# Dropping four unused columns from the output projection on, and cutting the last three token tiles from the other end

## The chip, the cores and the metric

The kernel runs on one core of a Trainium2 chip, which is trn2. The metric is the device time of one execution in microseconds; the median of three runs is used. The engines are TensorE (PE in the profile, its weight loads PEld), VectorE (DVE), ScalarE (ACT), GpSimd (POOL) and SyncE (SP), which here issues loads and stores.

## What is computed

One inference step of a one-layer encoder, for 1024 prompt tokens and 64 sample tokens that use the same weights. Cut to what matters here:

```
u = RMSNorm(x);  proj = u @ w_in
A = (RG-LRU branch with a width-4 causal conv) @ w_branch_a
B = (mLSTM branch with a width-4 causal conv) @ w_branch_b
x = x + (sigmoid(ga) * A + sigmoid(gb) * B) @ w_out
h = relu(RMSNorm(x) @ w_mlp_up)          # 1024 -> 4096
x = x + (h * h) @ w_mlp_down             # 4096 -> 1024
y = RMSNorm(x)
```

All values are fp32. The causal convolutions look three tokens back, and the sample's convolution starts from a given state.

## The kernel before

Activations lie transposed in SBUF: 128 rows of a feature block on the partitions, tokens as columns. There are KB = 8 feature blocks and COLS = 1092 columns: 1024 prompt tokens, a gap of GAP = 4 that the convolutions need for the sample's state, and 64 sample tokens from column SAMPLE0 = 1028 on. Up to the merge of the two branches every operation works on all 1092 columns, as three thirds of TW = 364 that fill three PSUM banks (slot_a, slot_b). A product in fp32 precision is made of three passes: operands and weights are split into a high and a low part, and hi x hi, hi x lo and lo x hi are added in PSUM. ScalarE makes the high parts, VectorE the low parts of activations, and GpSimd the low parts of weights.

The output projection `wo` makes eight products of 8 x 3 x 3 = 72 matmuls of 364 columns (weight_block, L849). `res_out(p)` on VectorE adds each to x, freeing its PSUM slot, with one tensor_tensor on 1092 columns. Behind it, ScalarE and VectorE make the operands of the MLP's first unit. Forms of three kinds (LATE) for the first three blocks are stored to DRAM and loaded again by SP (`late_forms`), because their place in SBUF is still in use. The tile late_z, from which one of them is stored, is part of the same SBUF space as raw21 and raw22s[0], where SP puts weights of the first MLP unit; `late22_11` waits for the stores (e_xy, e_zs) before it loads.

The MLP's up projection (4 groups) and the down projection of the first three groups are done as 2 x 2 block products with seven multiplications in place of eight (Strassen-Winograd). The columns are cut into two halves of HALF = 548, FIRST from 0 and SECOND up to 1092, which overlap by four. One of the seven products, `multiply(group, r, product, ready)`, has 4 blocks x 3 passes x 2 quarters = 24 matmuls of HT = 274 columns (L1107). There are 28 units of four groups each way, 7 products each, so 4704 matmuls in all, the first product of which stands apart at L1177. GpSimd combines and splits the weights of a unit (`sum1` to `sum4`, `lo`, L762 and L759), VectorE adds the products together (`partials`, `quarter`), and every engine's order is written out by hand, with semaphores between them.

The last group of the down projection is done as plain products, from last_x, an [8 blocks, hi and lo, COLS] operand that is loaded from DRAM (hid). It runs over three token tiles, LAST_TILES, of 512, 392 and 188 columns; a tile has 8 feature blocks of 24 matmuls (`last_term`, L1204), which go round four PSUM banks. TensorE may start a block when the one four before it has been drained (f_prod). For each block VectorE multiplies by the MLP's rstd, adds to acc and adds the square (`last_block`, `last_ssum`), and ScalarE squares and multiplies by the final gain (`final`). For a finished tile TensorE sums the squares over the partitions (`norm_tile`, L1196, after the second block of the tile that follows), ScalarE takes the root (L1922), VectorE the reciprocal (L2765), VectorE scales the tile (`last_y`), for the first tile together with GpSimd (L835, blocks 0 to 3), and SP stores it to y_d. Behind the last tile all of this stands in a row:

```
        last_ssum(TILES - 1, KB - 1)
        last_recip(TILES - 1)
        last_y(TILES - 1)
```

L1940, L1937 and L1247 are helpers through which most of VectorE's and ScalarE's operations are issued.

## Time and profile before

| | us |
|---|---|
| median of 3 runs | 2178.89 |
| lowest and highest run | 2176.95, 2181.11 |
| the profiled execution's own time | 2177.44 |
| its span | 2175.6 |
| TensorE busy | 2141.6 (98%) |
| VectorE busy | 1445.2 (66%) |
| GpSimd busy | 1099.7 (51%) |
| ScalarE busy | 715.4 (33%) |

The span is from the first to the last instruction or transfer of the profiled execution; all times in the rows below count from its start. The time of the execution holds 1.8 us more around it. A busy TensorE is not one at its peak: the recorded durations of its matmuls overlap, so the cost of one is read from starts, or from the chain of work.

### The profile page before, as it was taken

What the parts mean: (1) busy time and instruction counts of PE and PEld (TensorE: products, weight loads), DVE (VectorE), ACT (ScalarE), POOL (GpSimd) and SP (SyncE); (2) the same over time, 40 slices, a digit from 0 to 9 for tenths busy, and PEclk for the clock granted to TensorE, in tenths of its full rate; (3) what the DMA queues carried; (4) which work ended last, traced back from release to release, by engine and by line L of the source; (5) the groups of instructions that cost most, each with busy time, mean ns of one, the idle gap of its engine ahead of it and who ended that gap; (6) DMA issues with size and microseconds to landing.
All of it is one profiled execution on the core that took longest, in us unless ns stands there. A gap on an engine that the chain in (4) does not pass through costs nothing.

```text
span 2175.6 us, 37452 instructions
## 1 busy us (share of the span) xinstructions
PE 2141.6 (98%) x14230; PEld 2118.0 (97%) x14230; DVE 1445.2 (66%) x1509; ACT 715.4 (33%) x944; POOL 1099.7 (51%) x767
## 2 busy tenths in 40 slices
PE   7999999999999999999999999999999999999998
PEld 7999999999999999999999999999999999999988
DVE  6676776156767676867676755676978744456876
ACT  4433434213232332323232311234344433323332
POOL 3556565342434342333334244457777767688630
PEclk9999999999999999999999999999999999999999
DMA  3212213431212121111212132573545556627522
GB/s 132 67 57 59 67 55 93 151 98 55 67 44 66 46 74 57 54 57 49 66 44 66 44 105 85 177 243 134 198 164 199 171 195 225 233 93 260 178 60 83
DMA packets 96866, 237.83 MB, mean 109 GB/s; under 512 B 9457, under 2 KB 14705, under 8 KB 91921
## 3 DMA queue, kind: packets, MB, share of 16 engines
q1 hardware_dynamic: 58256, 109.58, 16.7%
q10 hardware_dynamic: 38528, 127.12, 16.2%
q8 instruction: 56, 0.92, 0.2%
q14 instruction: 26, 0.20, 0.0%
HBM read 172.18 MB, written 64.49 MB: 109 GB/s over the span
## 4 chain that ended last, share of the span: by engine, by line
PE 92%; DMA 3%; DVE 1%; ACT 1%; POOL 1%; issue 1%; ACTq 0%; SPq 0%; POOLq 0%; DVEq 0%
PE ps L849 55%; PE ps L1107 25%; PE ps L1204 5%; PE ps L1017 2%; PE ps L1050 2%; PE ps L1053 1%; PE ps L1032 1%; DMA form_lo<-hid_forms 1%; PE ps L1058 1%; PE ps L1004 1%; DMA rstd<-in_w 1%; DVE acc L1940 1%; DMA last_x<-hid 0%; DMA late_forms<-rstd 0%; PE ps L1005 0%
## 5 line engine op out<-in xcount | busy, mean ns | idle before, releaser
L739 POOL TENSOR_TENSOR w_hi<-w_raw,ones 128x512 fp32r<-128x512 f32 x218 | 263.0, 1206 | 815.4 <-PE ps L849 781.8
L849 PE MATMUL ps<-u_hi,w_hi 128*128 128x364 f32 x1560 | 347.8, 331 | 12.6 <-DVE u_lo L1937 9.8
L742 POOL TENSOR_TENSOR w_lo<-w_raw,w_hi 128x512 fp32r<-128x512 f32 x218 | 347.0, 1592 | 17.1
L849 PE MATMUL ps<-u_hi,w_lo 128*128 128x364 f32 x1560 | 345.2, 329 | 0.0
L849 PE MATMUL ps<-u_lo,w_hi 128*128 128x364 f32 x1560 | 344.7, 329 | 0.0
L849 PEld LDWEIGHTS ps<-u_hi,w_hi 128*128 128x128 f32 x1560 | 271.5, 189 | 13.6 <-issue 11.6
L849 PEld LDWEIGHTS ps<-u_lo,w_hi 128*128 128x128 f32 x1560 | 272.1, 189 | 0.0
L849 PEld LDWEIGHTS ps<-u_hi,w_lo 128*128 128x128 f32 x1560 | 272.0, 189 | 0.0
L1107 PE MATMUL ps<-form_hi,hi 128*128 128x274 f32 x784 | 164.0, 291 | 2.5 <-DMA form_lo<-hid_forms 1.0
L1107 PE MATMUL ps<-form_hi,w_hi 128*128 128x274 f32 x776 | 162.9, 291 | 1.4 <-POOL w_lo L759 0.9
L1107 PE MATMUL ps<-form_hi,lo 128*128 128x274 f32 x784 | 163.8, 290 | 0.0
L1107 PE MATMUL ps<-form_lo,hi 128*128 128x274 f32 x784 | 163.4, 290 | 0.0
L1107 PE MATMUL ps<-form_hi,w_lo 128*128 128x274 f32 x776 | 162.0, 290 | 0.0
L1107 PE MATMUL ps<-form_lo,w_hi 128*128 128x274 f32 x776 | 161.8, 290 | 0.0
L1940 DVE TENSOR_TENSOR acc<-acc 128x1092 f32<-128x1092 f32 (+2 forms) x72 | 109.0, 1527 | 34.4 <-ACT acc L1291 25.5
L1107 PEld LDWEIGHTS ps<-form_hi,hi 128*128 128x128 f32 x784 | 124.7, 190 | 3.2 <-issue 2.1
L1107 PEld LDWEIGHTS ps<-form_hi,w_hi 128*128 128x128 f32 x776 | 123.3, 190 | 2.4 <-issue 2.0
L1107 PEld LDWEIGHTS ps<-form_hi,lo 128*128 128x128 f32 x784 | 124.4, 189 | 0.0
L1107 PEld LDWEIGHTS ps<-form_lo,hi 128*128 128x128 f32 x784 | 124.3, 189 | 0.0
L1107 PEld LDWEIGHTS ps<-form_hi,w_lo 128*128 128x128 f32 x776 | 123.2, 189 | 0.0
L1107 PEld LDWEIGHTS ps<-form_lo,w_hi 128*128 128x128 f32 x776 | 123.0, 189 | 0.0
L1940 DVE TENSOR_TENSOR acc<-ps,acc 128x1092 f32<-128x1092 f32 x64 | 82.2, 1284 | 11.6 <-PE ps L849 11.6
(308 smaller groups left out, 4438.6 us busy)
## 6 DMA issues: line engine op xcount, KB each, us to landing
w_raw<-in_w SPq DMA_DIRECT2D x282, 256.0 KB, 2.6
form_lo<-hid_forms ACTq DMA_DIRECT2D x21, 1096.0 KB, 10.1
rstd<-in_w SPq DMA_DIRECT2D x50, 256.0 KB, 2.7
hid_forms<-acc ACTq DMA_DIRECT2D x12, 822.0 KB, 6.3
form_hi<-hid_forms ACTq DMA_DIRECT2D x9, 1096.0 KB, 7.7
bc<-out_rows ACTq DMA_DIRECT2D x8, 1092.0 KB, 6.1
hid_forms<-stage ACTq DMA_DIRECT2D x6, 1096.0 KB, 4.5
hid_forms<-acc ACTq DMA_DIRECT2D x12, 548.0 KB, 7.3
```

Of the source, the lines that this page charges most:

```text
L739: nc.gpsimd.tensor_tensor(w_hi[:, c, :], w_raw[:, c, :], one, ALU.mult).then_inc(s_whi, 1)
L742: nc.gpsimd.tensor_tensor(w_lo[:, c, :], w_raw[:, c, :], w_hi[:, c, :].bitcast(F32), ALU.subtract).then_inc(s_wlo, 1)
L849: mm = nc.tensor.matmul(slots[slot][:, t, :], w, r(k)[:, t * TW:(t + 1) * TW], start=(k == 0 and n == 0), stop=(k == last_k and n == 2))
L1004: nc.tensor.matmul(ps[:, 6 + c % 2, 0:n], kz[:, k0:k0 + CH], preq[:, t0:t0 + n], start=True, stop=True)
L1017: mm = nc.tensor.matmul(out, l, r, start=(cb == 0 and n == 0), stop=(cb == 1 and n == 2))
L1032: nc.tensor.matmul(ps[:, c % 2, 0:VW], kt[:, c % 2, :], vt3[:, c, :], start=True, stop=True).then_inc(m_u_mm, 1)
L1050: nc.tensor.matmul(out, vt3[:, c, j * P:(j + 1) * P], sw[:, c % 2, 0:n], start=True, stop=state is None)
L1053: nc.tensor.matmul(out, state[:, j * P:(j + 1) * P], bc[:, 1, t0:t0 + n], start=False, stop=True)
L1058: nc.tensor.matmul(ps[:, 3 + c % 2, 2 * P:2 * P + n], ones[:], (zw if c else sw)[:, c % 2, 0:n], start=True, stop=True).then_inc(m_o_mm, 1)
L1107: mm = nc.tensor.matmul(out[:, t, :], l, x[:, k, t * HT:(t + 1) * HT], start=(k == 0 and n == 0), stop=(k == 3 and n == 2))
L1204: return nc.tensor.matmul(ps[:, q % LAST_BANKS, 0:hi - lo], w, last_x[:, k, int(term == 2), lo:hi], start=first, stop=last)
L1940: V.tensor_tensor(out, in0, in1, op).then_inc(inc, 1)
```

## The change

From the output projection's result on, the four gap columns are no longer carried: MC = 1088. `res_out` leaves them out, with three instructions in place of one. HALF becomes 544 and the quarters 272 columns, the halves no longer overlap, and the residual, the hidden activations, the squares and the last operand have 1088 columns. The last tiles are [576, 1088), [236, 576) and [0, 236), in this order, so 512, 340 and 236 columns; the first of them holds the samples, and its stores are cut at the sample's first column. y_d keeps its 1092 columns. Nothing changes ahead of the output projection's drain.

```diff
-LAST_TILES = [(0, 512), (512, 904), (904, COLS)]
+MC = SEQ + DEC_SEQ
+LAST_TILES = [(576, MC), (236, 576), (0, 236)]
...
-HALF = (COLS + TAIL + 1) // 2
+HALF = MC // 2
 HT = HALF // 2
-FIRST, SECOND = slice(0, HALF), slice(COLS - HALF, COLS)
-NEW = slice(HALF, COLS)
-DUP = 2 * HALF - COLS
+FIRST, SECOND = slice(0, HALF), slice(HALF, MC)
...
-        last_x = sb_in(st, "last_x", [P, KB, 2, COLS], F32R)
-    sb("u_space", [P, 4 * 8 * HALF])
+        last_x = sb_in(st, "last_x", [P, KB, 2, MC], F32R)
+    sb("u_space", [P, 2 * KB * COLS])
...
-    rstd2 = sb("rstd2", [P, 2 * HALF])
+    rstd2 = sb("rstd2", [P, COLS])
...
-    squares = [tmp[:, 2, :]] * (KB - 1) + [stage[:, 1, 0:COLS]]
+    squares = [tmp[:, 2, 0:MC]] * (KB - 1) + [stage[:, 1, 0:MC]]
...
-    x2_d = nc.dram_tensor("residual", (KB, P, COLS), F32, kind="Internal").ap()
+    x2_d = nc.dram_tensor("residual", (KB, P, MC), F32, kind="Internal").ap()
...
-    hid_d = nc.dram_tensor("hid", (KB, P, COLS), F32, kind="Internal").ap()
+    hid_d = nc.dram_tensor("hid", (KB, P, MC), F32, kind="Internal").ap()
...
-                sp.dma_start(y_d[js, :, lo:hi].rearrange("j p c -> p j c"), acc[:, js, lo:hi]).then_inc(s_out, 16)
-        sp.wait_ge(s_out, 16 * (4 + TILES + 1))
+                for c0, c1, at in ((lo, min(hi, SEQ), lo), (SEQ, hi, SAMPLE0)):
+                    if c0 < c1:
+                        sp.dma_start(y_d[js, :, at:at + c1 - c0].rearrange("j p c -> p j c"), acc[:, js, c0:c1])\
+                            .then_inc(s_out, 16)
+        sp.wait_ge(s_out, 16 * (4 + TILES + 3))
...
-            tt(as3(acc[:, n, :]), slots[half], as3(tmp[:, half, :]), ALU.add, s_dr[half])
+            whole = 2 * TW
+            two = lambda ap: ap.rearrange("p (a b) -> p a b", a=2)
+            V.tensor_tensor(two(acc[:, n, 0:whole]), slots[half][:, 0:2, :], two(tmp[:, half, 0:whole]), ALU.add)
+            V.tensor_tensor(acc[:, n, whole:SEQ], slots[half][:, 2, 0:SEQ - whole], tmp[:, half, whole:SEQ], ALU.add)
+            tt(acc[:, n, SEQ:MC], slots[half][:, 2, SAMPLE0 - whole:TW], tmp[:, half, SAMPLE0:COLS], ALU.add, s_dr[half])
...
             if half:
-                tt(acc[:, n, NEW], acc[:, n, NEW], part[:, DUP:HALF], ALU.add, h_add)
+                tt(acc[:, n, SECOND], acc[:, n, SECOND], part, ALU.add, h_add)
```

The other lines put MC, or 0:MC, where COLS or the whole row stood: in the sums of squares, the mean square's last product and its copy, the reciprocal, the stores of x2 and hid and the row operations of the residual.

## Rows read from the trace of the kernel before

**Rows 1.** The page, busy time, share of the span and instructions.

```profile
PE 2141.6 (98%) x14230; PEld 2118.0 (97%) x14230; DVE 1445.2 (66%) x1509; ACT 715.4 (33%) x944; POOL 1099.7 (51%) x767
```

**Rows 2.** The page, the chain that ended last by engine.

```profile
PE 92%; DMA 3%; DVE 1%; ACT 1%; POOL 1%; issue 1%; ACTq 0%; SPq 0%; POOLq 0%; DVEq 0%
```

**Rows 3.** Busy us by stretch: length, engines, granted clock, DMA share, GB/s.

```profile
core 0: us, PE busy (x) PEld busy (x) DVE busy (x) ACT busy (x) POOL busy (x), PEclk, DMA share, GB/s
1452.00:1483.60 31.60, 28.69 (x220) 27.88 (x218) 25.68 (x22) 14.12 (x23) 24.25 (x17) 1.00 0.66 229
1483.60:1966.70 483.10, 483.10 (x3776) 481.94 (x3777) 310.49 (x302) 186.98 (x296) 364.65 (x249) 1.00 0.52 182
1500.00:1600.00 100.00, 100.00 (x786) 100.00 (x785) 85.23 (x79) 41.23 (x70) 77.27 (x52) 1.00 0.55 191
```

**Rows 4.** TensorE's waits from 1400 us on: total us, times, longest.

```profile
PE ps L1196 <- DVE tmp L1940: 1.6, 1, 1.6
PE ps L1204 <- ACT last_x L1247: 1.5, 2, 1.0
...
PE ps L1107 <- DMA form_lo<-hid_forms: 1.0, 1, 1.0
```

**Rows 5.** The chain in order of time: start us, length us, what.

```profile
1213.06 3.54 PE ps L1017 x30
...
1233.66 0.22 PE ps L1050 x2
...
1236.27 192.18 PE ps L849 x1152
...
1428.53 1.31 DVE acc L1940
...
1519.41 447.28 PE ps L1107 x3504
...
2116.49 0.86 PE ps L1196 x2
...
2148.34 0.68 PE ps L1196 x2
```

**Rows 6.** Timeline of TensorE in the last stage: start us, first start to last end.

```profile
2084.06 21.04 PE L1204 MATMUL ps<-last_x,last_w 128*128 128x512 f32 x90
2104.93 0.63 PE L1204 MATMUL ps<-last_x,hi 128*128 128x512 f32 x2
...
2107.73 0.52 PE L1204 MATMUL ps<-last_x,w_hi 128*128 128x392 f32 x2
...
2142.84 0.36 PE L1204 MATMUL ps<-last_x,w_hi 128*128 128x188 f32 x2
...
2164.80 0.27 PE L1204 MATMUL ps<-last_x,lo 128*128 128x188 f32 x1
```

**Rows 7.** Timeline of VectorE in the last tile.

```profile
2155.32 2.60 DVE L2765 RECIPROCAL rstd<-rstd 128x392 f32<-128x392 f32 x1
...
2158.70 3.42 DVE L1940 TENSOR_TENSOR acc<-acc,rstd 128x3136 f32<-128x3136 f32 x1
...
2162.41 0.35 DVE L1940 TENSOR_TENSOR acc<-acc,tmp 128x188 f32<-128x188 f32 x1
2162.69 0.35 DVE L1940 TENSOR_TENSOR tmp<-tmp 128x188 f32<-128x188 f32 x1
...
2165.11 0.35 DVE L1940 TENSOR_TENSOR tmp<-ps,tmp 128x188 f32<-128x188 f32 x1 [1.17 <-PE ps L1204]
...
2167.76 1.33 DVE L2765 RECIPROCAL rstd<-rstd 128x188 f32<-128x188 f32 x1 [1.13 <-ACT rstd L1922]
2169.20 1.73 DVE L1940 TENSOR_TENSOR acc<-acc,rstd 128x1504 f32<-128x1504 f32 x1
```

**Rows 8.** By stretch, as rows 3: the output stores of the last two tiles.

```profile
2163.00:2168.00 5.00, 2.66 (x21) 2.20 (x20) 2.48 (x9) 2.66 (x7) 0.00 (x0) 1.00 0.88 321
2171.00:2175.00 4.00, 0.00 (x0) 0.00 (x0) 0.00 (x0) 0.00 (x0) 0.00 (x0) 0.50 0.61 193
```

**Rows 9.** By stretch, as rows 3: behind TensorE's wait for last_x.

```profile
2063.20:2067.00 3.80, 3.80 (x10) 2.97 (x11) 3.80 (x3) 2.40 (x5) 3.72 (x3) 0.55 0.52 133
```

More of the change, by code:

```diff
@@ L676, in row @@
                 sp.wait_ge(f_row, 2 * (n - 2) + 2)
-            sp.dma_start(stage[:, n % 2, 0:COLS], x2_d[n]).then_inc(g_in[n % 2], 16)
+            sp.dma_start(stage[:, n % 2, 0:MC], x2_d[n]).then_inc(g_in[n % 2], 16)
         first_weights()
@@ L1119, in mean_square @@
             else:
-                nc.tensor.matmul(ps[:, b, 0:COLS - 2 * BANK], ones[:], tmp[:, 3, 2 * BANK:COLS], start=True, stop=True)\
+                nc.tensor.matmul(ps[:, b, 0:MC - 2 * BANK], ones[:], tmp[:, 3, 2 * BANK:MC], start=True, stop=True)\
                     .then_inc(s_norm, 1)
@@ L1565, in square @@
         def square(p):
-            a(squares[p], acc[:, ROWS[p], :], ACT.Square, s_sq)
+            a(squares[p], acc[:, ROWS[p], 0:MC], ACT.Square, s_sq)
         def keep(n):
-            act.dma_start(x2_d[n], acc[:, n, :]).then_inc(o_st, 16)
+            act.dma_start(x2_d[n], acc[:, n, 0:MC]).then_inc(o_st, 16)
         def late_store(f, part, j, src, inc):
@@ L1657, in norm_out @@
             for src, lo, hi in (((ps[:, b, :], 0, BANK), (ps[:, b + 1, :], BANK, 2 * BANK)) if r == 1 else
-                                ((ps[:, b, 0:COLS - 2 * BANK], 2 * BANK, COLS),)):
+                                ((ps[:, b, 0:MC - 2 * BANK], 2 * BANK, MC),)):
                 a(tmp[:, 3, lo:hi], src, ACT.Identity, n2_dr, scale=1.0 / D_MODEL, bias=eps_c[:, 0:1])
@@ L1673, in store_last @@
             rows = slice(2 * r, 2 * r + 2)
-            act.dma_start(hid_d[r:KB:4].rearrange("b p c -> p b c"), acc[:, rows, :]).then_inc(h_st[r % 2], 16)
+            act.dma_start(hid_d[r:KB:4].rearrange("b p c -> p b c"), acc[:, rows, 0:MC]).then_inc(h_st[r % 2], 16)
         def relu2(group, r, i):
@@ L2439, in res_ssum @@
             dve.wait_ge(s_sq, KB + p + 1)
-            tt(tmp[:, 3, :], tmp[:, 3, :], squares[p], ALU.add, s_ssum)
+            tt(tmp[:, 3, 0:MC], tmp[:, 3, 0:MC], squares[p], ALU.add, s_ssum)
             dve.wait_ge(s_ssum, KB - 1 + p + 1)
@@ L2595, in recip @@
         def recip(step):
-            w = slice(step * COLS // 3, (step + 1) * COLS // 3)
+            w = slice(step * MC // 3, (step + 1) * MC // 3)
             dve.wait_ge(n2_dr, 3)
@@ L2694, in row @@
             dve.wait_ge(g_in[n % 2], 128 + 16 * (n // 2) + 16)
-            tt(acc[:, n, :], acc[:, n, :], tmp[:, 3, :], ALU.mult, f_row)
+            tt(acc[:, n, 0:MC], acc[:, n, 0:MC], tmp[:, 3, 0:MC], ALU.mult, f_row)
             dve.wait_ge(f_row, 2 * n + 1)
-            tt(acc[:, n, :], acc[:, n, :], stage[:, n % 2, 0:COLS], ALU.add, f_row)
+            tt(acc[:, n, 0:MC], acc[:, n, 0:MC], stage[:, n % 2, 0:MC], ALU.add, f_row)
         for group in range(UP_GROUPS + 1, ALL_GROUPS):
```

## Prediction

> **What bounds the kernel now.** I read the page's busy times first [rows 1]: TensorE is busy for 98% of the span, and the chain that ended last runs through it for 92% [rows 2]. The reader is to see that no other engine comes near; a change pays only where it shortens TensorE's own stream, or where TensorE waits.
>
> Next I cut the span into stages [rows 3]. The 483 us from 1483.6 on (the MLP's units) have TensorE busy without a gap, while a hundred of them near the start have VectorE busy for 85 and GpSimd for 77. The 31.6 us ahead of them (the hand-over from the output projection to the MLP) hold only 28.7 us of TensorE work. The waits of TensorE from 1400 us on [rows 4] are few, the longest of them 1.6 us in the tail, 1.5 us on ScalarE's last operands and 1.0 us on a load of stored forms.
>
> Third, the chain in order of time gives the cadence, start to start, which the busy times do not, since a matmul's recorded duration overlaps its successor's. From [rows 5]: 3504 matmuls of 274 columns in 447.28 us, 127.6 ns each; 1152 of 364 columns in 192.18 us, 166.8 ns; 30 of 256 columns in 3.54 us, 118 ns; two of 128 columns in 0.22 us, 110 ns. From the starts in the last stage [rows 6]: 90 of 512 columns between 2084.06 and 2104.93, 232 ns. The 392-column tile runs from 2107.73 to 2142.84, less 0.86 us of a norm product inside it, over 192 matmuls: 178.4 ns. The 188-column tile runs from 2142.84 to 2164.80 plus one cadence of 0.11, less 0.68 us, over 192: 111.4 ns. So from 274 to 364 columns a column costs 39.2/90 = 0.436 ns, and below some 240 columns the cadence is flat at 110 to 111 ns: 128 and 188 columns cost the same. These two facts carry the prediction.
>
> **The change, part by part.**
>
> *MLP products, 274 to 272 columns.* HALF goes from 548 to 544, each product is still 24 matmuls, and there are 28 units of 7 products, 4704 matmuls. Up to 1483.6 us the products' starts are set by others (below), which takes some 240 matmuls out. The remaining 4464 save 2 x 0.436 = 0.87 ns each: **-3.89 us**. By the array's plain rate at full clock, 1/2.4 ns a column, it would be -3.72. Nothing else becomes the limit: VectorE's work shrinks in the same proportion (548 to 544), GpSimd's is unchanged at 77 of 100 us. The first-half/second-half overlap of four columns disappears; the add that skipped it already had 544 elements, so it costs the same.
>
> *The output projection's drain (res_out), one VectorE instruction into three.* It took 1.31 us on 1092 columns [rows 5]. Each instruction more costs its start: consecutive 188-column adds start 0.28 us apart [rows 7], of which 188 x 1.04 = 0.20 us is elements, so 0.085 us each, 0.17 us for two, and -0.004 for four columns. It happens eight times. TensorE needs a slot only a whole product (12 us) later, so seven are hidden. One is not: from the drain at 1428.53 the chain [rows 5] goes through VectorE's forms, two stores of late forms out of the tile that the next weight load overwrites, that load, and GpSimd's sums and splits, and ends in the wait that TensorE leaves at 1483.59. Behind it VectorE's seven or so operations lose 4 ns each. I take **+0.15 us** (bounds: 0 if a DMA's jitter covers it, 0.5 if two drains count). In this stretch the faster matmuls save nothing, since GpSimd and the loads pace it.
>
> *Last tiles, 512/392/188 to 512/340/236.* The 512 tile is as it was. At 340 columns the line between 274 and 364 gives 166.8 - 24 x 0.436 = 156.3 ns, 22.1 ns less over 192 matmuls: **-4.24 us**. At 236 columns the line gives 111.0, just where the flat part is; I take 112 ns: **+0.10 us**, with an upper bound at the 118 ns of 256 columns, +1.27. The norm product of the middle tile goes from 0.68 to some 0.60 us (0.86 at 512): **-0.08**. So TensorE loses columns where they cost and gets them where they are free.
>
> Here a rule speaks against the change. The Trainium skill (TensorE: Matmul & The Clock Gate, section Back-to-back issue gap) gives an isolated matmul as N/2.4 + 2.5 ns, estimated 81 ns at 188 columns and 101 at 236; by that alone the two tiles together would gain only 0.3 us, and the whole sum would be about -2.5 us. The trace shows 111.4 ns at 188 columns, so it does not agree; the page's own weight-load time of P/1.2, 107 ns for 128 columns, fits the floor that the rows show.
>
> *VectorE in the last tile.* It must not fall behind. Before, it waited 1.17 us for TensorE's last block [rows 7]. Now its reciprocal of the middle tile takes 6.2 ns (from 2.60 and 1.33 us at 392 and 188 columns) x 52 = 0.32 us less, the scaling of eight blocks 416 x 1.04 = 0.43 us less, and three to four blocks in that stretch 0.17 us more each: the slack stays near 1.1 us. Hidden; no term.
>
> *The tail after the last matmul*, a chain of one operation after the other, now on 236 columns. Three tensor_tensor of 48 more elements: 0.15. Square, norm product and square root at 0.05 each (an estimate from the same slope): 0.15. Reciprocal 48 x 6.2 ns: 0.30. The scaling, 8 x 48 elements at (3.42 - 1.73)/1632 = 1.04 ns: 0.40. Together **+1.00 us**. Then the output store, 944 instead of 752 KB. The DMA share [rows 8] is 5 x 0.88 = 4.4 us for the middle tile's 1568 KB and 4 x 0.61 = 2.4 us for the last one's 752 KB, 2.4 ns per KB: **+0.46 us** (0.3 to 0.7).
>
> *Transfers and queues.* x2, hid, the forms and the last operands shrink by 0.4 to 0.7%; loads behind the three DMA waits gain under 0.1 us, about as much as the shorter cover loses. The first tile now holds the samples, so its two stores on SP's queue become four, some 40 us before the end; SP waits there for nothing but the later tiles, whose stores it issues long after. No term. The SBUF tiles move by a few bytes under operations of the same shape; no row speaks for a gain or a loss, and I give that nothing.
>
> **Sum.** -3.89 + 0.15 - 4.24 + 0.10 - 0.08 + 1.00 + 0.46 = -6.5 us. Against the profiled execution's 2177.44 us (span 2175.6) that is 2170.9; the median of the three runs is 1.45 us higher, so 2178.89 - 6.5 = **2172.4 us**, 0.3% less. A measurement can tell about 0.2%, 4.4 us.
>
> **Rivals.**
>
> A coarser step. If columns are read in fours, 274 counts as 276 and two further columns are saved: 4464 x 0.87 = 3.9 us more, -10.4, 2168.5 us. If in eights, 274 counts as 280: 11.7 us more, -18.2, 2160.7 us. For it: 127.6 ns lies 0.5 to 1.5 ns above lines drawn through the other sizes, all of them multiples of four. Against: the line from 392 to 512 columns (54/120 = 0.45) and that from 364 to 392 (0.41) scatter as much. Chance 0.12.
>
> The MLP's cadence does not move, because something per matmul and not per column sets it. For: at 188 columns it is just so. Against: 274 lies 17 ns above that floor. Then -2.6 us, 2176.3: no change. With another engine pacing the MLP, which would give the same (against it VectorE's 85 of 100 us), chance 0.08.
>
> The last tile pays for its columns: 48 x 0.436 ns x 192 = 4.0 us in place of 0.10, the sum is -2.6 us, again 2176.3. For: 236 columns lie where the slope would begin. Against: 128 and 188 columns cost the same, and even 256 only 118 ns. Chance 0.02. (The page's N/2.4 + 2.5, by an estimate, gives this case.)
>
> The other side: the clock. When TensorE idled for 1.5 us before the last stage, the granted clock fell, to 0.55 on the mean of the next 3.8 us [rows 9], that is from 2.4 to 1.2 GHz for most of them, and these cost about 1.7 us (0.45 x 3.8). At the hand-over TensorE now idles 2.9 us in several gaps, at a granted clock of 1.00 [rows 3]. If the longer drain lengthens them enough for the clock to fall there until the stream is whole at 1483.6, up to 28 us run at the half rate and lose up to 14 us, net +7.5, 2186 us. It decides once more than 6.5 + 4.4 = 10.9 us are lost, 22 us at the low level. Against: the gaps grow by 0.15 us in all. Chance 0.03.
>
> **How the numbers follow.** My forecast has 0.75. Its own range: with every bound against it (118 ns, +0.5, a store of 0.7, tail 1.2, tile one 0.3 worse, plain rate) -3.9; with all for it -7.4; with the scatter of a median of runs that lie 4 us apart, 2170.5 to 2176. The overall range adds the step in fours below: 2166.5 to 2176.3; the step in eights, the clock and the edge of the unmoved cadence stay outside. Faster by over 0.2%: 0.65 of the forecast's 0.75 and the 0.12 of the step, 0.77. Within 0.2%: the rest of the forecast, 0.10, and the two rivals at 2176.3, 0.10, so 0.20. Slower: 0.03.
>
> **What would show it.** In the profile after: some 3500 matmuls of 272 columns without a break at 126.7 ns (the term is wrong if 127.6; 125.9 or 124.0 means a step); 192 matmuls of the middle tile in 30.0 us and of the last in 21.5 us without the norm products; the first unbroken MLP product starting about 55.2 us after the drain of the sixth block began, against 55.06; 7.0 us from TensorE's last block to the end of the final scaling, against 6.0 (2164.9 to 2170.9), and 5.1 us from there to the span's end, against 4.7. It would be wrong if TensorE shows new waits on tmp or acc in the last tile, a fallen clock after 1455 us, or 236-column matmuls above 118 ns.

## The result, and the profile after

The change makes the kernel 0.65% faster: median 2165.14 us (2162.93 to 2168.36, four runs) against 2178.78 for the kernel before beside it (four runs), ratio 0.9935 [0.9922, 0.9947]. That is 13.6 us less, where the prediction had 6.5 us less, and below the low end of its range. The profiled execution took 2165.02 us (span 2163.1) against 2177.44 (span 2175.6). A second measurement of the changed kernel gave 0.9933, so the size is not an accident of one. One of the eleven runs of the kernel with 276 columns below took 3518 us at a mean granted clock of 0.56, and is left out of that kernel's ratio.

The page of the kernel after, busy times and the chain that ended last, beside [rows 1, 2]:

```profile
PE 2125.1 (98%) x14230; PEld 2102.0 (97%) x14230; DVE 1446.8 (67%) x1525; ACT 715.3 (33%) x944; POOL 1102.7 (51%) x767
...
PE 93%; DMA 2%; DVE 2%; POOL 1%; ACT 1%; issue 1%; SPq 0%; ACTq 0%; POOLq 0%; DVEq 0%
```

TensorE sets the time as before, with the same number of matmuls. VectorE has 16 instructions more, the two for each of eight drains.

The chain in order of time, beside [rows 5] (start us, length us, what):

```profile
1485.80 12.29 PE ps L1109 x96
...
1521.07 454.83 PE ps L1109 x3624
...
1989.84 63.48 PE ps L1109 x504
2053.32 21.08 PE ps L1206 x90
...
2106.84 27.52 PE ps L1206 x192
2134.36 0.57 PE ps L1198 x2
2134.93 16.33 PE ps L1206 x144
```

The second line is the one to read: 454.83/3624 is 125.5 ns a matmul, where [rows 5] give 447.28/3504, 127.65. The prediction had 126.7. The difference looks small, but it is multiplied by 4464 matmuls. The other five traces with 274 columns, taken for the experiments below, read 127.55 to 127.6, and five more with 272 in the changed kernel's layout 125.5, so a cadence repeats within 0.1 ns.

By stretch, beside [rows 3, 9]:

```profile
core 0: us, PE busy (x) PEld busy (x) DVE busy (x) ACT busy (x) POOL busy (x), PEclk, DMA share, GB/s
1454.00:1485.80 31.80, 27.24 (x212) 26.45 (x211) 25.94 (x25) 13.76 (x23) 22.78 (x15) 1.00 0.65 226
1485.80:1975.90 490.10, 490.10 (x3896) 489.05 (x3897) 320.74 (x310) 193.16 (x304) 375.53 (x256) 1.00 0.52 191
1500.00:1600.00 100.00, 100.00 (x798) 99.90 (x797) 86.12 (x79) 42.04 (x71) 77.94 (x51) 1.00 0.53 190
```

In a hundred microseconds TensorE now does 798 matmuls in place of 786, and VectorE and GpSimd are busy a little longer for it (86.1 and 77.9 us). The granted clock at the hand-over is 1.00, in spite of 4.6 us without matmuls there.

TensorE's waits from 1400 us on, beside [rows 4]:

```profile
PE ps L1109 <- issue: 2.9, 1, 2.9
PE ps L1109 <- DMA form_lo<-hid_forms: 1.9, 1, 1.9
PE ps L1198 <- DVE tmp L1942: 1.8, 1, 1.8
```

The wait for last_x, 1.5 us in [rows 4], is gone, and with it the fall of the clock behind it. The last stage in TensorE's timeline, beside [rows 6]:

```profile
2053.16 2.15 PE L1206 MATMUL ps<-last_x,w_hi 128*128 128x512 f32 x8
...
2098.41 0.47 PE L1206 MATMUL ps<-last_x,w_hi 128*128 128x340 f32 x2
...
2128.78 0.38 PE L1206 MATMUL ps<-last_x,w_hi 128*128 128x236 f32 x2
...
2150.97 0.27 PE L1206 MATMUL ps<-last_x,lo 128*128 128x236 f32 x1
```

From these starts, the drain of the sixth block and the span's end, both executions fall into the same six stages:

| stage, us | before | after | predicted change | change |
|---|---|---|---|---|
| to the drain of the sixth block (code not touched) | 1428.53 | 1429.57 | 0 | +1.04 |
| hand-over, to the first unbroken product | 55.06 | 56.23 | +0.15 | +1.17 |
| MLP, to the first 512-column matmul | 575.98 | 567.36 | -3.89 | -8.62 |
| first tile, 512 columns | 48.16 | 45.25 | 0 | -2.91 |
| middle tile | 35.11 | 30.37 | -4.24 | -4.74 |
| last tile, tail and store | 32.76 | 34.32 | +1.48 | +1.56 |

The first two are scatter between executions: of two further profiles, the kernel before had 54.36 in the second stage and the kernel after 54.64, and the end of the first lies anywhere from 1427.4 to 1431.7 in the other traces. Without them the table gives -14.7 us. So there are two questions: why the MLP gave twice its term, and where the first tile's gain comes from.

### The profile page after: what moved, and what is told of

Same layout as the page of the kernel before. It is cut to its first block, busy times and chain, and to the rows that moved or that the text cites. A ratio compares the mean times of both kernels' runs of the same rounds, so it can differ in the third digit from the quotient of the medians.

```text
span 2163.1 us, 37470 instructions
## 1 busy us (share of the span) xinstructions
PE 2125.1 (98%) x14230; PEld 2102.0 (97%) x14230; DVE 1446.8 (67%) x1525; ACT 715.3 (33%) x944; POOL 1102.7 (51%) x767
## 4 chain that ended last, share of the span: by engine, by line
PE 93%; DMA 2%; DVE 2%; POOL 1%; ACT 1%; issue 1%; SPq 0%; ACTq 0%; POOLq 0%; DVEq 0%
PE ps L851 55%; PE ps L1109 26%; PE ps L1206 4%; PE ps L1019 2%; PE ps L1052 2%; PE ps L1055 1%; PE ps L1034 1%; PE ps L1060 1%; DVE acc L1942 1%; PE ps L1006 1%; DMA rstd<-in_w 1%; DMA form_lo<-hid_forms 1%; PE ps L1007 0%; POOL w_lo L761 0%; ACT vt L1488 0%
## 5 line engine op out<-in xcount | busy, mean ns | idle before, releaser
L1109 PE MATMUL ps<-form_hi,hi 128*128 128x272 f32 x784 | 162.1, 288 | 5.2 <-issue 2.9
L1109 PE MATMUL ps<-form_hi,w_hi 128*128 128x272 f32 x776 | 161.2, 289 | 1.3 <-POOL w_lo L761 1.3
L1109 PE MATMUL ps<-form_hi,lo 128*128 128x272 f32 x784 | 162.3, 288 | 0.0
L1109 PE MATMUL ps<-form_lo,hi 128*128 128x272 f32 x784 | 161.9, 288 | 0.0
L1109 PE MATMUL ps<-form_lo,w_hi 128*128 128x272 f32 x776 | 160.5, 288 | 0.0
L1109 PE MATMUL ps<-form_hi,w_lo 128*128 128x272 f32 x776 | 160.4, 288 | 0.0
L1942 DVE TENSOR_TENSOR snap<-ps,snap 128x544 f32<-128x544 f32 x72 | 51.5, 716 | 57.9 <-PE ps L1109 57.6
```

Of the source, the lines that this page charges most:

```text
L1109: mm = nc.tensor.matmul(out[:, t, :], l, x[:, k, t * HT:(t + 1) * HT], start=(k == 0 and n == 0), stop=(k == 3 and n == 2))
L1942: V.tensor_tensor(out, in0, in1, op).then_inc(inc, 1)
```

## The experiments

**The kernel before, a second trace.** No edit.

> The kernel before once more, unchanged, for a second trace. If the two waits of the first trace at the start of the last stage (1.5 us for the last operand, and 3.8 us at a granted clock of 0.55) are part of this kernel, they come again. If they are the scatter of one execution, the last stage begins without them, and about 3 us of the difference between the two kernels' traces belong to no part of the change. The 274-column cadence stays at 127.6 ns, and the MLP's unbroken run starts 55 to 57 us after the sixth block's drain begins.

2176.25 us. The MLP took 577.36 us, the hand-over 54.36, the first tile 46.15. So two of the 2.9 us that the first tile seems to gain belong to that one trace, in which the clock fell [rows 9]. Here TensorE waited 1.0 us for last_x, in two waits of 0.5, as its timeline shows:

```profile
2062.76 0.50 PE L1204 MATMUL ps<-last_x,w_hi 128*128 128x512 f32 x1 [0.52 <-ACT last_x L1247]
2063.76 0.50 PE L1204 MATMUL ps<-last_x,w_hi 128*128 128x512 f32 x1 [0.50 <-ACT last_x L1247]
```

**One width for each of the seven products**, in the kernel after and, as the same edit on the other layout, in the kernel before:

```diff
# columns, start of the first and of the second quarter; in the kernel after:
+cols, first, second = {P5: (272, 0, 272), P6: (270, 0, 272), P2: (268, 0, 272), P7: (264, 0, 272), P1: (256, 0, 272), P3: (268, 2, 274), P4: (268, 4, 276)}[product]
# in the kernel before:
+cols, first, second = {P5: (274, 0, 274), P6: (272, 0, 274), P2: (272, 0, 276), P7: (270, 0, 274), P1: (268, 0, 274), P3: (264, 0, 274), P4: (256, 0, 274)}[product]
...
-                        mm = nc.tensor.matmul(out[:, t, :], l, x[:, k, t * HT:(t + 1) * HT],
+                        c0 = (first, second)[t]
+                        mm = nc.tensor.matmul(out[:, t, 0:cols], l, x[:, k, c0:c0 + cols],
```

> The changed kernel with the seven products of every MLP unit cut to 272, 270, 268, 264 and 256 columns, and two more of 268 that start 8 and 16 bytes into the row; the columns left out are not computed. If the cadence goes by columns at 0.42 to 0.44 ns each, it reads 125.5, 124.6, 123.8, 122.0 and 118.5 ns. If it goes in steps of four columns, 270 costs what 272 costs (125.5), and 268, 264 and 256 are 1.7 ns lower for each four. If it goes in steps of eight or more, 268 costs 125.5 too and 264 falls by 3.5 or more. If what counts is where the row of 272 starts, the shifted 268 differ from the plain one; by columns alone all three are the same.

> The kernel before with its products cut to 274, 272, 272 (second quarter from column 276), 270, 268, 264 and 256 columns, in its own rows of 548; the columns left out are not computed. If the number of columns alone made the changed kernel faster, 272 columns run at 125.5 ns here too, 2.1 ns below 274, with either start. If it is the place of the rows or of the second quarter (column 274 starts 8 bytes off a multiple of 16), 272 columns read 126.7 ns or more with the start at 274, and 125.5 only with the start at 276. By a plain price per column 272 is 0.87 ns below 274 in both.

2161.15 and 2163.23 us, one execution each. Neither computes the columns that are left out. The medians over the products, as the distance of one product's start from the next divided by 24: in the kernel after 125.0 ns at 272 columns, 125.4 at 270, 124.2 at 268, 121.9 at 264, 118.1 at 256. The two further products of 268 columns differ: with both quarters shifted by 8 bytes 126.2, with both shifted by 16 bytes 123.5. In the kernel before 127.8 at 274, 125.8 at 272 with the second quarter from column 274, 124.8 at 272 with it from column 276, 125.9 at 270, 124.1 at 268, 122.9 at 264, 119.4 at 256. From the timeline of the first:

```profile
1610.23 0.41 PE L1111 MATMUL ps<-form_hi,hi 128*128 128x272 f32 x2
...
1613.22 0.41 PE L1111 MATMUL ps<-form_hi,hi 128*128 128x270 f32 x2
...
1616.20 0.41 PE L1111 MATMUL ps<-form_hi,w_hi 128*128 128x268 f32 x2
...
1619.18 0.41 PE L1111 MATMUL ps<-form_hi,w_hi 128*128 128x264 f32 x2
...
1624.95 0.41 PE L1111 MATMUL ps<-form_hi,hi 128*128 128x268 f32 x2
...
1627.98 0.41 PE L1111 MATMUL ps<-form_hi,w_hi 128*128 128x268 f32 x2
...
1630.92 0.41 PE L1111 MATMUL ps<-form_hi,w_hi 128*128 128x272 f32 x2
```

2.99, 2.98 and 2.98 us for 24 matmuls: from 272 to 268 columns next to nothing is saved, while from 274 to 272 it is 2.0 to 3.0 ns in the other kernel. The curve is not a line, and a slope read over 90 columns doesn't hold for a step of two. It could seem that width alone, in steps, explains all of it. But the start of an operand shows too: the same 268 columns take 3.03 us when shifted by 8 bytes (from 1624.95 on) and 2.94 when shifted by 16, and in the kernel before the two products of 272 columns, with different starts of the second quarter, lie 1.0 ns apart. These are different products, and in a kernel of one width the seven products differ among themselves by 0.6 to 1.0 ns, so this is a sign and not a price.

**Wider than 272.** The same kind of edit in the kernel after, with 272, 276, 280, 284, 288, 278 and 274 columns, all second quarters from column 256. The quarters overlap, so that what it computes is not the reference's.

> The changed kernel with the seven products of every MLP unit widened to 272, 276, 280, 284, 288, 278 and 274 columns (the second quarter starts at column 256, so that the columns overlap and the numbers are not the reference's). From the narrower widths (118.3 ns at 256, 121.9 at 264, 124.3 at 268, 125.0 at 270 and 272, 127.6 at 274 in the kernel before) a step of eight predicts 125.0 at 272, one level of 128 for 274, 276, 278 and 280, and one of 131.5 for 284 and 288. By a plain price of 0.43 per column it is 125.5, 126.4, 127.2, 128.1, 129, 130.7 and 132.4 ns in order of width.

2179.95 us, one execution. From the timeline:

```profile
1614.18 0.43 PE L1111 MATMUL ps<-form_hi,hi 128*128 128x272 f32 x2
1617.22 0.42 PE L1111 MATMUL ps<-form_hi,hi 128*128 128x276 f32 x2
1620.26 0.41 PE L1111 MATMUL ps<-form_hi,w_hi 128*128 128x280 f32 x2
1623.33 0.42 PE L1111 MATMUL ps<-form_hi,w_hi 128*128 128x284 f32 x2
...
1629.67 0.42 PE L1111 MATMUL ps<-form_hi,hi 128*128 128x278 f32 x2
1632.75 0.42 PE L1111 MATMUL ps<-form_hi,w_hi 128*128 128x274 f32 x2
1635.84 0.42 PE L1111 MATMUL ps<-form_hi,w_hi 128*128 128x272 f32 x2
```

Medians: 126.3 ns at 272, 128.5 at 274, 127.3 at 276, 129.4 at 278, 128.6 at 280, 131.4 at 284, 132.8 at 288. Now 274 and 278 lay above their neighbours, as though widths that are no multiple of four paid for the next one. A product measured among others of other widths is a weak witness, though: 272 columns read between 124.8 and 126.3 in the three kernels. So the next kernels have one width throughout.

**All products at 272 columns, nothing else moved** (the kernel before, second quarter still from column 274; the last two columns of each quarter are not computed):

```diff
-out[:, t, :], l, x[:, k, t * HT:(t + 1) * HT]
+out[:, t, 0:HT - 2], l, x[:, k, t * HT:(t + 1) * HT - 2]
```

> The kernel before, its rows, halves, transfers and tiles untouched, with each quarter's matmul cut from 274 to 272 columns; the last two columns of each quarter are not computed. If the width of the matmul alone made the MLP faster, its cadence is 125.4 to 125.5 ns and the time 4464 x 2.1 to 2.2 = 9.5 us below the kernel before, 0.9956, within what its waits scatter. If smaller transfers and vector work carried part of it, it stays above 0.997. By a plain 0.44 ns per column it is 3.9 us, 0.9982.

2174.30 us, 0.9972 [0.9959, 0.9986]: 5.0 us less than the kernel before by the medians (2179.32), 6.1 by the ratio, from the width alone. The chain's row:

```profile
1520.30 439.28 PE ps L1107 x3480
```

126.2 ns, where 125.4 to 125.5 was expected: the width alone gives 1.4 ns of the 2.15.

**All products at 276 columns** (the kernel before, second quarter from column 272, so that its numbers are not the reference's):

```diff
-out[:, t, :], l, x[:, k, t * HT:(t + 1) * HT]
+ps[:, 2 * s + t, 0:HT + 2], l, x[:, k, t * (HT - 2):t * (HT - 2) + HT + 2]
```

> The kernel before with each quarter's matmul widened from 274 to 276 columns, the second starting at column 272, so that more is computed (and the second quarter's numbers are not the reference's). If what costs in 274 is that it is no multiple of four, 276 columns run at 126.9 to 127.2 ns, 0.5 to 0.7 ns below 274, and the kernel does more in 2 to 3 us less, 0.9987. If the price is one per column, it is 128.5 ns and 4 us more, 1.0018. If the cost is that of a step of eight, 276 and 274 are alike, 1.000.

2182.83 us, 1.0014 [1.0001, 1.0028]:

```profile
1519.79 447.02 PE ps L1107 x3480
```

128.45 ns. This ends both steps: 276 costs 0.8 ns more than 274, where steps of four and of eight wanted them equal. The second quarter's start differs too (column 272, against 274 in the kernel before). The next kernel shows the start at 272 to be the cheaper one at 272 columns, so that is no reason for 276 to cost more.

**All products at 272 columns, second quarter from column 272** (byte 1088 in place of 1096), otherwise as the kernel at 272 above; the last four columns of a half are not computed:

```diff
-out[:, t, :], l, x[:, k, t * HT:(t + 1) * HT]
+out[:, t, 0:HT - 2], l, x[:, k, t * (HT - 2):(t + 1) * (HT - 2)]
```

> The kernel before with quarters of 272 columns as in the run that gave 126.2 ns, but the second one starting at column 272 instead of 274 of its row (the last four columns of a half are not computed). The pitch of the rows has been shown not to matter (125.5 ns at either). If the 0.7 ns is the second quarter's start, 1096 bytes into the row, no multiple of 16, against 1088, the cadence is 125.5 ns here. If it stays at 126.2, it belongs to something else that the changed kernel does differently, the vector work's lengths or places.

2166.49 us in one execution, against 2179.49 for the kernel before beside it. Its chain:

```profile
1519.09 352.70 PE ps L1107 x2808
```

125.6 ns, what the kernel after has (125.5), in the layout of the kernel before. The start of the second quarter is worth 0.6 ns of the rest. All seven products are faster than with the start at 274, by 0.4 to 1.2 ns (medians over the units).

**The other half of that question: the kernel after with rows of 548 in place of 544** under its forms and last operands.

```diff
+ROW = HALF + 4
...
-        last_x = sb_in(st, "last_x", [P, KB, 2, MC], F32R)
+        last_x = sb_in(st, "last_x", [P, KB, 2, 2 * ROW], F32R)[:, :, :, 0:MC]
...
-        high = [[sb_in(st, f"form{f}_{part}", [P, 4, HALF], F32R) for part in ("hi", "lo")] for f in range(4, FORMS)]
+        high = [[sb_in(st, f"form{f}_{part}", [P, 4, ROW], F32R)[:, :, 0:HALF] for part in ("hi", "lo")] for f in range(4, FORMS)]
```

> The changed kernel, everything computed, with the rows of its operand tiles in SBUF (the seven forms and last_x) set 548 columns apart again in place of 544, so 2192 bytes in place of 2176; quarters stay at 272 columns, the second starts at 272. In the kernel before, cut to 272 columns, the cadence was 126.2 ns, in the changed kernel it is 125.5. If the rows' pitch is the 0.7 ns, it is 126.2 here; if it is the second quarter's start (column 274 or 272), or the drains and adds of VectorE that go along, it stays at 125.5. Between these it would be both.

2170.83 us in one execution: its MLP took 576.3 us, with TensorE waiting for VectorE (2.4 us once, 1.9 us in five) and for a load of stored forms (2.2 us). But the unbroken stretch says what was asked:

```profile
1517.92 271.11 PE ps L1110 x2160
```

125.5 ns: in the MLP the distance of rows costs nothing. In the last stage it is not so. There the rows of last_x lie 4384 bytes apart in place of 4352, and the same two tiles read otherwise than in the kernel after:

```profile
2103.98 0.47 PE L1207 MATMUL ps<-last_x,w_hi 128*128 128x340 f32 x2
...
2134.65 0.38 PE L1207 MATMUL ps<-last_x,w_hi 128*128 128x236 f32 x2
...
2140.76 16.11 PE ps L1207 x144
```

The 340-column tile takes 30.67 us against 30.37, 155.3 ns a matmul against 153.7. The 236-column tile has 16.11/144 = 111.9 ns against 16.33/144 = 113.4. The two nearly cancel.

**The last tiles alone**, in the kernel before, twice:

```diff
-LAST_TILES = [(0, 512), (512, 904), (904, COLS)]
+LAST_TILES = [(580, COLS), (240, 580), (0, 240)]
```

> The kernel before with only the last token tiles changed, to 512, 340 and 240 columns from the end; halves of 548 and 1092 columns everywhere. My prediction gave the tiles -4.24 + 0.10 - 0.08 + 1.00 + 0.46 = -2.8 us. From the two traces (35.1 to 30.4 us, 22.1 to 22.3, tail 10.7 to 12.0) it is -3.2 us, so a ratio of 0.9985 to 0.9987. If the last stage's start belongs to the first tile's place (columns 576 on instead of 0 on), it is 3 us more, 0.997. If the middle tile's columns were free too, nothing: 1.000.

> The kernel before with the new tiles alone, a second trace. In its first one TensorE did not wait for last_x ahead of the last stage, as in no trace of the changed kernel, while the three traces with the old tiles and 1092 columns had 1.0 to 1.5 us of it. If the tiles remove the wait, it is absent again; nothing ahead of the last stage depends on them, so I expect it back at 0.5 to 1.0 us, as a matter of one execution. The middle tile takes 30.6 us and what follows it 34.4 us, as the first time.

First 2175.62 us against 2178.92, 0.9989 [0.9976, 1.0001] (by the ratio 2.4 us less), then 2176.30 in one execution. Middle tile 30.61 and 30.62 us, the rest 34.41 and 34.27: 2.9 us less than the 67.87 of the kernel before (tiles, tail and store were priced at 2.8 less). The first of the two had no wait for last_x, the second had one of the three longest of all:

```profile
PE ps L1204 <- ACT last_x L1247: 1.9, 2, 1.4
```

So the order of the tiles, which puts the samples into the first one, doesn't remove that wait.

**The widths alone**: the kernel after with the old tiles.

```diff
-LAST_TILES = [(576, MC), (236, 576), (0, 236)]
+LAST_TILES = [(0, 512), (512, 904), (904, MC)]
```

> The changed kernel (1088 columns, quarters of 272) with the tiles cut as before, 512, 392 and 184 columns from the start. If the quarters carry the gain at 2.1 ns a matmul (9.6 us over 4464), and with them half a us to 3 us of shorter waits, it is 9 to 12 us below the kernel before, 0.9945 to 0.996; by a plain price per column, 3.9 us, 0.998. The difference to the changed kernel is the tiles', 3 us.

2171.39 us, 0.9964 [0.9950, 0.9979], 7.8 us less by the ratio. MLP 566.61 us, middle tile 35.04. Its end holds something that the change as a whole doesn't pay. The last operation of its VectorE timeline:

```profile
2158.96 1.69 DVE L1942 TENSOR_TENSOR acc<-acc,rstd 128x1472 f32<-128x1472 f32 x1
```

From its end at 2160.65 to the span's end at 2166.8 are 6.2 us; the kernel before, with four columns more to store, took 4.7. With the old order the samples lie in the last tile and are stored by a second DMA, issued 0.4 us behind the first, after everything else: 1.5 us more. In the order from the end they are stored 40 us earlier. The prediction counted these two further stores and called them "no term"; that is right only because the tiles are turned round.

**The drain in three alone**, in the kernel before (728, 296 and 68 columns).

> The kernel before with only the output projection's drain cut into three instructions (728, 296 and 68 columns). By the prediction the handover grows by 0.15 us and the time does not move (ratio 1.000, within 0.001). If the handover's 1.2 us longer in the changed kernel's trace comes from the drain, the MLP's unbroken run starts 56.2 us after the sixth block's drain begins, against 55.06, and the time is 1 us above.

2179.58 us, 1.0007 [0.9997, 1.0016]. Its hand-over took 53.90 us, the shortest but one of all traces. Whether the two instructions are hidden or cost 0.15 us, nothing shows.

**Tiles of 336 and 240**, in the kernel after, with a second measurement of the kernel after beside it:

```diff
+LAST_TILES = [(576, MC), (240, 576), (0, 240)]
```

> The changed kernel once more, for a second trace and a closer time. From the earlier runs of its halves, the tiles alone (0.9989) and the columns alone (0.9964), it should be 0.995 of the kernel before, 10 to 11 us below, where the first comparison gave 0.9935 (0.9922 to 0.9947). If the missing wait before the last stage was the scatter of one execution, it is there in this trace again or not, and the time scatters by 3 us with it. The MLP's cadence is 125.5 ns.

> The changed kernel with the middle and last tile cut to 336 and 240 columns, both multiples of eight, in place of 340 and 236. If a matmul's cost goes up in steps of eight columns, 340 costs what 344 would, and the middle tile gains 192 times 2 to 3 ns, 0.4 to 0.6 us, while the last one stays at 113 ns and the tail gains 0.1 us; in all 0.3 to 0.6 us below the changed kernel, which only the stages of the trace can show. By columns alone 4 x 0.436 x 192 = 0.33 us. If 240 columns left the floor, it would be slower.

The kernel after: 2165.09 us, 0.9933 [0.9921, 0.9946], where its two halves, measured apart, had let 0.995 be expected. With 336 and 240: 2167.42, 0.9939 [0.9926, 0.9952], the same within the intervals. Middle tile 30.29 us (30.37 at 340), rest 34.24 (34.32). Four columns between 336 and 340 are worth 0.4 ns (153.3 and 153.7), or 0.1 ns a column; between 272 and 276 they are worth 2.9. The MLP took 573.3 us in this trace, 6 more than in the others of the changed kernel, and lost them in waits such as these:

```profile
1811.44 0.70 PE L1109 MATMUL ps<-form_hi,w_hi 128*128 128x272 f32 x2 [3.00 <-DVE acc L1942]
...
1993.94 0.49 PE L1109 MATMUL ps<-form_hi,hi 128*128 128x272 f32 x2 [2.25 <-POOL w_lo L761]
```

**Rows of the DRAM tensors.** The stores of late forms land sooner in the kernel after, and the hand-over's waits had changed places. Two kernels put the old distance of rows (548 and 1092 elements) under the kernel after, and rows at a multiple of 64 bytes under the kernel before:

```diff
# in the kernel after
+    late_d = nc.dram_tensor("late_forms", (18, P, HALF + 4), F32, kind="Internal").ap()[:, :, 0:HALF]
+    hid_d = nc.dram_tensor("hid", (KB, P, COLS), F32, kind="Internal").ap()[:, :, 0:MC]
# in the kernel before
+    late_d = nc.dram_tensor("late_forms", (18, P, HALF + 12), F32, kind="Internal").ap()[:, :, 0:HALF]
+    hid_d = nc.dram_tensor("hid", (KB, P, COLS + 12), F32, kind="Internal").ap()[:, :, 0:COLS]
```

> The changed kernel with the rows of two DRAM buffers (the late forms and the hidden activations of the last group) set 2192 and 4368 bytes apart instead of 2176 and 4352, so that they no longer start at multiples of 64 bytes; what is moved is the same. In all traces so far the 548-column kernels' stores of late forms land in 3.6 to 4.0 us and those of 544 in 2.9 to 3.1, seven times the difference of their sizes. If that is the place of the rows, they are back at 3.6 to 4.0 here; if not, they stay at 3.0. The load of last_x took 8.0 to 8.2 us in most traces before and 6.5 to 7.0 after: it goes to 8 if the pitch sets it.

> The kernel before with the rows of the same two DRAM buffers set 2240 and 4416 bytes apart, multiples of 64, in place of 2192 and 4368; what is moved is the same. If the place of the rows sets the time of a store, the late forms' stores fall from 3.6 to 4.0 us to about 3.0, and the waits of the hand-over take the pattern of the changed kernel (0.36 and 1.8 us in place of 0.5, 0.8 and 0.7). If the load of last_x and TensorE's wait of 1.0 to 1.5 us before the last stage hang on it, the load takes 6.5 us and the wait is 0.5 us or none.

2161.86 us and 2186.95 us, one execution each. The page's row of the first store (KB each, median us from issue to landing) in the kernel after, and in it with the old distance:

```profile
late_forms<-rstd ACTq DMA_DIRECT2D x9, 272.0 KB, 3.1
```

```profile
late_forms<-rstd ACTq DMA_DIRECT2D x9, 272.0 KB, 3.4
```

In the other six traces of the changed layout this figure is 2.9 to 3.0, so the old distance may cost 0.3 us, on one trace. The kernel before with the aligned distance has 3.6, and the nine other traces of its layout 3.6 to 4.0: aligning the longer rows shows nothing. The hand-over took 54.89 us with the old distance, as in other traces; no link between these stores and its length shows. And with 2.6 us the kernel with aligned rows waited longest of all for last_x, so alignment is not what removed this wait either.

## Why the prediction was right in kind and wrong in size

**What bounds the kernel: right.** TensorE alone, without a gap in the MLP.

**The MLP's term, -3.89 us: the step that failed.** It rested on "from 274 to 364 columns a column costs 39.2/90 = 0.436 ns" and applied this mean slope to a step of two columns. The mechanism was right (fewer columns, a faster stream, no other engine taking over), the size was not: 2.15 ns a matmul in place of 0.87, 9.6 us over 4464 in place of 3.9. The stage as a whole bears this out: its median is 576.7 us in six traces with 274 columns (575.8 to 580.3) and 567.3 in six of the changed layout with 272 (four at 566.5 to 567.4, the two with the new waits named above at 573.3 and 576.3). The runs divide the 2.15 ns: the width alone gives 127.65 to 126.2 (4464 x 1.4 is 6.3 us; 5.0 to 6.1 were timed), the start of the second quarter 126.2 to 125.6, and the distance of rows nothing. The prediction gave the moved addresses nothing, as "no row speaks for a gain or a loss"; that was the second thing missing, 4464 x 0.6, 2.7 us of the term.

Near 272 the curve is steeper and rough: 125.5 ns at 272, 127.65 at 274, 128.45 at 276. From 276 to 364 columns a column again costs 0.436 ns. At 272 the cadence lies 1.2 ns under that line with the second quarter from column 272, and 0.5 under it with the start at 274. The kernel of 274 columns lies on the line, but it carries the start at 274 with it; 274 columns with a better start were not run. The sweeps at mixed widths put 272 above 268 by 0.7 to 1.7 ns and above 264 by 1.9 to 3.1. Why the engine prices widths and starts so was not found. With 5.7 us the miss on this term is most of the 7.3 us by which the forecast was off.

**The rival "a coarser step": near in number, wrong in mechanism.** Its 125.9 ns for fours is close to the 125.5 of the trace, and the kernel with mixed widths from 272 up spoke for it. 276 columns at 128.45 ns, in a kernel of one width, refute it: by fours 276 would cost what 274 does. Without that kernel the document would tell a story that fits.

**Middle tile, -4.24 and -0.08 us: right**, -4.74 in the trace. 153.7 ns against 156.3 from the same straight line, again cheaper than the line has it (0.5 us). About half of that goes with the place of the rows: 340 columns read 154.9 ns with rows of 1092 columns (the tiles alone) and 155.3 with rows of 1096.

**Last tile, +0.10: right in kind, a little low.** 113.2 ns at 236 columns against the 112 chosen, so +0.2 us more; with the norm product of 0.57 us 22.30 us in all. The rule weighed against this part, the Trainium skill's N/2.4 + 2.5 ns for an isolated matmul (TensorE: Matmul & The Clock Gate, section Back-to-back issue gap), does not fit the new sizes either: an estimated 101 ns at 236 columns and 116 at 272, where the rows show 113.2 and 125.5. The two tiles gained 4.5 us together in TensorE's stream, not the 0.3 that it gives.

**Tail and store, +1.46: right**, +1.33. The timeline of VectorE after TensorE's last block, beside [rows 7]:

```profile
2151.28 0.40 DVE L1942 TENSOR_TENSOR tmp<-ps,tmp 128x236 f32<-128x236 f32 x1 [1.49 <-PE ps L1206]
...
2154.25 1.63 DVE L2771 RECIPROCAL rstd<-rstd 128x236 f32<-128x236 f32 x1 [1.25 <-ACT rstd L1924]
2155.98 2.12 DVE L1942 TENSOR_TENSOR acc<-acc,rstd 128x1888 f32<-128x1888 f32 x1
```

7.02 us from 2151.08 to the end at 2158.10, where 7.0 was said; reciprocal +0.30 and scaling +0.39, within a hundredth as priced; 5.00 us of store against 5.1. VectorE's slack in this tile grew a little (it waited 1.49 us, [rows 7] 1.17), so nothing came from that side.

**The drain, +0.15: right.** Of the sixth block:

```profile
1429.57 0.92 DVE L2451 TENSOR_TENSOR acc<-ps,tmp 128x728 f32<-128x728 f32 x1 [5.14 <-PE ps L851]
1430.40 0.46 DVE L2452 TENSOR_TENSOR acc<-ps,tmp 128x296 f32<-128x296 f32 x1
1430.77 0.21 DVE L1942 TENSOR_TENSOR acc<-ps,tmp 128x64 f32<-128x64 f32 x1
1431.02 1.60 DVE L1939 SCALAR_TENSOR_TENSOR tmp<-acc,small,tmp 128x544 f32<-128x544 f32 x1
```

The next operation starts 1.45 us after the drain began, 1.33 before: 0.12 us more. What a hand-over takes varies by 2.3 us over the kernels run (53.90 to 56.23, without the one in which the clock fell, next paragraph), so 0.15 is below what it can show, and the kernel with the drain alone says the same.

**The clock: did not fall, but the rival was a real one.** TensorE stood still for 4.6 us at the hand-over in place of 2.9, 2.94 of them in one piece, and the granted clock stayed at 1.00:

```profile
1478.07 0.49 PE L1109 MATMUL ps<-form_hi,hi 128*128 128x272 f32 x2 [2.94 <-issue]
...
1485.80 0.49 PE L1109 MATMUL ps<-form_hi,w_hi 128*128 128x272 f32 x2 [0.97 <-POOL w_lo L761]
```

In the kernel after with the mixed widths it did fall there: behind 1.97 us of idle TensorE the granted clock was 0.53 on the mean of the next 3.5 us, so 1.2 GHz for most of them. With slower matmuls there was no further wait for weights, and the stream is unbroken from 1478.98 on, 47.3 us after the drain began. Before the last stage the clock fell in two traces, after 1.5 us of waits (0.55) and after 2.6 us (0.57), and not in two others, after 1.9 and 2.0 us. So the length of the pause alone does not tell whether it falls.

**The first tile, no term: 1 to 3 us gained, cause narrowed but not found.** TensorE's wait for last_x goes with the width of the MLP's products rather than with the layout. In the eight traces whose products have 274 columns or more on the mean it is 1.5, 1.0, 1.1, 0, 1.9, 1.4, 2.6 and 2.0 us. In the ten with 272 or fewer it is 0, 0, 0, 0, 0.5, 0.5, 0.8, 0.8, 0.5 and 0.5. The last of the eight is the kernel after with widths from 272 up:

```profile
PE ps L1208 <- ACT last_x L1251: 2.0, 2, 1.5
```

The last three of the ten are in the layout of the kernel before. That is 1.4 us against 0.4 on the mean, plus the clock in two of the eight (first tile 48.2 and 49.3 us, elsewhere 44.8 to 47.3). With it goes the load of last_x: 8.0 to 8.8 us from issue to landing in seven of the eight, 6.5 in the one without a wait, and 6.4 to 7.4 in the ten. The order of tiles and aligned rows are excluded as the cause. Why the load is shorter when the products are narrower was not tested.

**Adding up.** By the ratios the tiles alone gave 2.4 us and the widths alone 7.8, and the widths alone paid 1.5 us for samples stored last: 11.7, where both at once give 14.5 (by the medians of the second measurement, 0.9933). Each ratio is uncertain by some 3 us, and the traces need nothing more (9.6 from the MLP, 2.9 from the tiles with their tail, about 1 from the first tile: 13.5). Whether a small interaction is left, these runs don't tell.

One sum in the prediction is off: its forecast's own range, with the bounds as they are given, is -4.1 to -6.8 and not -3.9 to -7.4. The overall range does not hang on it.

## What to carry to other kernels

A cadence is to be read at the widths that are used, in a kernel of that one width: the slope over 90 columns gave 0.87 ns for a step of two that gave 2.15, start included, and over thousands of matmuls that was 5.7 us. Before trusting a step rule that fits, run the width that it calls equal; and where an edit moves an operand's start, give that a bound of its own, even if no row prices it. The rest of such a change (a drain in more pieces, a longer tail after a wider last tile, a floor under the narrow one) is priced well from durations in the trace.

## What the runs showed of the hardware that was not expected

- TensorE at a granted clock of 1.00, 128 rows, streams of this kernel, ns a matmul start to start: 110 at 128 columns, 111.4 at 188, 113.2 at 236, 125.5 at 272, 127.65 at 274, 128.45 at 276, 153.3 at 336, 153.7 at 340, 166.8 at 364, 178.4 at 392, 232 at 512. Between neighbouring sizes a column costs 0.1 (336 to 340) to 0.7 ns (272 to 276).
- The second of two operand slices from byte 1096 of its row in place of 1088 cost 0.6 ns a matmul at 272 columns (126.2 and 125.6). At 268 columns both slices from 8 bytes further on read 126.2 ns and from 16 bytes further on 123.5, where the unshifted product had 124.2 (mixed widths, different products). The Trainium skill (SBUF — State Buffer, section Operand start alignment) asks only for a multiple of the element size, which all these starts are, and says that its runs timed nothing; here the start shows in the time.
- The distance of the operand's rows cost nothing at 272 columns (125.5 ns at 2176 and at 2192 bytes), but at 4384 bytes in place of 4352 it went with 1.6 ns more at 340 columns and 1.5 less at 236. Other tiles moved with it, so which address counts was not told apart.
- Stores of rows of 2176 bytes landed after 2.9 to 3.1 us (late forms, first store, seven traces), those of 2192 bytes, under 1% more, after 3.6 to 4.0 (nine traces). The shorter row at the old distance had 3.4, the longer one at an aligned distance 3.6. Two such stores stand in the chain of the hand-over (4.02 and 3.65 us in the kernel before, 3.36 and 2.62 in the kernel after), but the hand-over was no shorter: 53.9 to 56.2 us in the one layout, 54.3 to 56.2 in the other (without the kernel in which the clock fell there).
